# The first pair of each feed-forward stage by eight plain products, late token sums, and filters at full width

## The reference

```python
def encoder_layer(x, lp):
    x = x + 0.5 * swiglu(rms_norm(x, lp['norm_ffn1']), lp['ffn1_w_in'], lp['ffn1_w_out'])
    h = rms_norm(x, lp['norm_mix'])
    proj = h @ lp['w_in']
    ...
    x = x + mixed @ lp['w_out']
    x = x + 0.5 * swiglu(rms_norm(x, lp['norm_ffn2']), lp['ffn2_w_in'], lp['ffn2_w_out'])
    return x

def swiglu(x, w_in, w_out):
    gate, up = jnp.split(x @ w_in, 2, axis=-1)
    return (jax.nn.silu(gate) * up) @ w_out

def hyena_filters(seq_len, lp):
    ...
    h = jnp.sin(freq * (z @ lp['hy_ff_w1'].astype(f32) + lp['hy_ff_b1'].astype(f32)))
    h = jnp.sin(freq * (h @ lp['hy_ff_w2'].astype(f32) + lp['hy_ff_b2'].astype(f32)))
    h = (h @ lp['hy_ff_w3'].astype(f32)).reshape(seq_len, 2, HY_ORDER, C_DIM)
    ...
    h = h * jnp.exp(-t * jnp.abs(deltas))[:, None, None, :]
    h_fwd, h_bwd = h[:, 0], h[:, 1]
    kern = jnp.concatenate([h_fwd, jnp.zeros((1, HY_ORDER, C_DIM), f32), jnp.flip(h_bwd[1:], axis=0)], axis=0)
    return kern / jnp.sum(jnp.abs(kern), axis=0, keepdims=True)
```

## Time and profile before

| | |
|---|---|
| median of 3 executions | 3457.19 us (3455.61 to 3460.02) |
| the profiled execution | 3455.17 us, of which the span is 3453.4 us |
| PE busy | 3263.6 us, 95% of the span |
| DVE, ACT, POOL busy | 2488.0, 1316.1, 74.9 us |
| matmuls of the pairs (L1064) | 7392 in three groups of 2464 |
| mean granted clock of TensorE | 0.984 of full speed |

### The profile page before, as it was taken

The page is one execution under the profiler, slowest core; times in us unless marked ns, Lnnn a source line. Parts: engine busy times, 40 slices in busy tenths (PEclk is TensorE's granted clock), DMA queues, the critical chain, the costliest instruction groups (busy, mean ns, idle before and its releaser), DMA issues.

```text
span 3453.4 us, 63597 instructions
## 1 busy us (share of the span) xinstructions
PE 3263.6 (95%) x25876; PEld 3063.6 (89%) x25876; DVE 2488.0 (72%) x4660; ACT 1316.1 (38%) x2491; POOL 74.9 (2%) x112
## 2 busy tenths in 40 slices
PE   5999999999898999999989999999999978999998
PEld 5899999888776989999979999998877768999997
DVE  7777777663878677667887777776548776776666
ACT  5333334221445343333543333351234535333333
POOL 0001000000000000000000000000000000000000
PEclk8999999999999999999999999999999999999999
DMA  2222222222033112222212222232310512222222
...
DMA packets 89553, 268.15 MB, mean 78 GB/s; under 512 B 10184, under 2 KB 18376, under 8 KB 87984
## 3 DMA queue, kind: packets, MB, share of 16 engines
...
## 4 chain that ended last, share of the span: by engine, by line
PE 81%; DVE 13%; issue 3%; ACT 2%; DMA 1%; SPq 0%; DVEq 0%; POOL 0%; ACTq 0%
PE ps L980 47%; PE ps L1064 34%; DVE uv L2809 1%; DVE wl L2288 1%; DVE gated L2334 1%; DMA wring<-wa 1%; DVE x L2196 0%; DVE rstd L2158 0%; DVE ps L2323 0%; DVE silu L2324 0%; PE ps L1528 0%; DVE gl L2427 0%; DVE gated L2329 0%; DVE wl L2149 0%; DVE act_low L2340 0%
## 5 line engine op out<-in xcount | busy, mean ns | idle before, releaser
L1064 PE MATMUL ps<-gh,wh 128*128 128x384 f32 x2464 | 833.5, 338 | 63.6 <-DVE wl L2288 25.9
L1064 PE MATMUL ps<-gl,wh 128*128 128x384 f32 x2464 | 829.6, 337 | 0.0
L1064 PE MATMUL ps<-gh,wl 128*128 128x384 f32 x2464 | 829.4, 337 | 0.0
L1064 PEld LDWEIGHTS ps<-gh,wh 128*128 128x128 f32 x2464 | 467.5, 190 | 73.0 <-DVE wl L2288 21.8
L980 PE MATMUL ps<-act_high,wh 128*128 128x384 f32 x1408 | 482.0, 342 | 11.3 <-DVE act_low L2340 11.1
L980 PE MATMUL ps<-act_high,wl 128*128 128x384 f32 x1408 | 473.0, 336 | 0.0
L980 PE MATMUL ps<-act_low,wh 128*128 128x384 f32 x1408 | 472.9, 336 | 0.0
L1064 PEld LDWEIGHTS ps<-gl,wh 128*128 128x128 f32 x2464 | 467.4, 190 | 0.4
L1064 PEld LDWEIGHTS ps<-gh,wl 128*128 128x128 f32 x2464 | 467.3, 190 | 0.0
L2196 DVE SCALAR_TENSOR_TENSOR x<-ps,x 128x384 f32<-128x384 f32 x416 | 229.2, 555 | 227.6 <-PE ps L980 227.2
L1661 ACT CAST wh<-wring 128x512 fp32r<-128x512 f32 (+2 forms) x260 | 182.9, 706 | 455.8 <-PE ps L980 368.4
...
## 6 DMA issues: line engine op xcount, KB each, us to landing
wring<-wa SPq DMA_DIRECT2D x244, 512.0 KB, 3.5
wring<-wa SPq DMA_DIRECT2D x128, 256.0 KB, 2.6
...
bias<-bias SPq DMA_DIRECT2D x24, 512.0 KB, 7.6
...
table<-hyc POOLq DMA_DIRECT2D x12, 512.0 KB, 4.0
kern_rows<-kst POOLq DMA_DIRECT2D x24, 256.0 KB, 3.1
outT<-x SPq DMA_DIRECT2D x2, 3072.0 KB, 9.7
```

The source lines that it names most:

```text
L1064: m = pe.matmul(out, lhs[a], rhs[b], start=start and n == 0, stop=stop and n == 2, skip_group_check=onto)
```

## The change

- The first pair of each stage, and all three pairs of the first block in stage 1, is made by eight plain products (`eight`, `plain_product`, `plain_pair`): two of each of four units of weights (the halves of the gate and up tiles as they are, no sums), with B11, T1, B2 and B2. The first half of the tokens leaves the bank as it is; the second adds the held product of B11.
- T2 (with T4's sum), T3 and T4 are made during the first pairs (`LATE_SUMS`): in stages 2 to 4 behind products 4 and 6 of the first pair and behind product 1 of the second, in stage 1 in its second and third pair. T3 no longer comes from T2 but from x and the scaled first tokens, which ACT makes again ("z").
- The filters are made for both orders at once, 256 columns wide: half as many jobs, at new places; sums of magnitudes go to bank 0, kernels to banks 2 and 3; `kst` and `kodd` lie where `silu1` and `gated1` are. `table` lies where `small` and the masks are, so these are loaded in each layer after the last filter, behind the store of x. At the start the second tile of weights is loaded after x.
- Waits are by name of the event instead of by a count worked out from the number of the pair; PE's wait for `small` at L1615 is not touched.

```diff
+def eight(l, f, j):
+
+    return j < (FF_BLOCKS[0][1] if l + f == 0 else 1)
+
+
+def units_of(l, f, j):
+    return 4 if eight(l, f, j) else UNITS
+
+
+def products_of(l, f, j):
+    return 8 if eight(l, f, j) else UNITS
...
-    jobs = [(0, ("mlp", 1)), (4, ("mlp", 2)), (4, None)]
-    for h, o, s in TAP_GROUPS:
-        jobs += [(1, ("taps", h, o, s, p)) for p in TAP_TILES[s][::2]] + [(3, ("sum", h, o, s))]
-        jobs += [(4 if n else 1, ("kern", h, o, a)) for n, a in enumerate(KERN_ORDER[o, s])]
+    jobs = [(2, ("mlp", 1)), (4, ("mlp", 2)), (3, None)]
+    for h, s in TAP_GROUPS:
+        jobs += [(1, ("taps", h, s, p)) for p in TAP_TILES[s][::2]] + [(3, ("sum", h, s))]
+        jobs += [(5 if n else 1, ("kern", h, a)) for n, a in enumerate(SEG_FOLDS[s])]
     out, at = {}, 0
     for gap, job in jobs:
         at += gap
-        if at % 16 > 13:
+        if at % 16 > 12:
...
+        def eight_banks(l, f, j):
+
+            return (4, 5, 6, 7) if j % 2 else (0, 1, 2, 3 if l + f == 0 else 6)
+
+        LATE_SUMS = {(0, 0, 1, 4): "T2", (0, 0, 1, 6): "T3", (0, 0, 2, 4): "T4"}
+        for l_, f_ in PASSES[1:]:
+            LATE_SUMS.update({(l_, f_, 0, 4): "T2", (l_, f_, 0, 6): "T3", (l_, f_, 1, 1): "T4"})
+        PLAIN_LEAD = (3, 3, 3, 3, 5, 5, 6, 6)
+        PLAIN_PARTS = (0, 1, 3, 5)
+        PLAIN_NAMES = ("B11", "T1", "B2", "B2")
...
+            def load_small(l):
+                sp.wait_ge(*fp.at(l, *FILTER_JOBS[-1]))
                 sp.dma_start(small[:, :], small_d[l]).then_inc(s_small, 16)
+                sp.dma_start(cs("masks"), const_d[:, COFF["masks"]:COFF["masks"] + 512]).then_inc(s_masks, 16)
...
                 sp.dma_start(x[:, i:KT:KH, :], xT[:, i:KT:KH, :]).then_inc(s_x[i], 16)
-                if i == 0:
-                    load_tile(1)
-            sp.dma_start(cst[:, :], const_d).then_inc(s_const, 16)
+            load_tile(1)
             load_tile(2)
-            sp.dma_start(small[:, :], small_d[0]).then_inc(s_small, 16)
+            sp.dma_start(cst[:, 512:], const_d[:, 512:]).then_inc(s_const, 16)
...
                 sp.wait_ge(s_xup, x_count(l, 0) + FF_OUTS)
                 sp.dma_start(outT, x[:, :, :]).then_inc(s_spill, 16)
+                load_small(l)
...
                         for dr in range(2):
-                            lo = CHH * (2 * dr + o)
-                            m = mm(ps[:, p % 2, CHH * dr:CHH * dr + CHH], h1[0:64, fold_tokens(p)], hwt[0:64, lo:lo + CHH])
-                        m.then_inc(*fp.inc(l, "taps", h, o, p))
+                            c = slice(2 * CHH * dr, 2 * CHH * dr + 2 * CHH)
+                            m = mm(ps[:, p % 2, c], h1[0:64, fold_tokens(p)], hwt[0:64, c])
...
+            def plain_product(l, f, j, p):
+
+                i, c = p // 2, p % 4
+                pe.wait_ge(*ul.at(l, f, j, i))
+                high, low = unit_part(wh, l, f, j, i), unit_part(wl, l, f, j, i)
+                for k in range(KH):
+                    if j == 0:
+                        pe.wait_ge(*eg.at(2 * l + f, k, PLAIN_NAMES[c]))
+                    gh, gl, _, at = pair_part(k, PLAIN_PARTS[c])
+                    m = mm3_onto(bank(eight_banks(l, f, j)[p // 4 * 2 + p % 2], HALF), (high[:, k, :], low[:, k, :]),
+                                 (gh[:, at, :], gl[:, at, :]), k == 0 and c < 2, k == KH - 1, c > 1)
+                m.then_inc(*pr.inc(l, f, j, p))
+
+            def banks_left(l, f, j, *last):
+
+                pe.wait_ge(*ex.at(l, f, j, *(last or ("u1" if eight(l, f, j) else "u0",))))
+
+            def plain_pair(l, f, j):
+                if pair_before(l, f, j) and pair_before(*pair_before(l, f, j)):
+                    banks_left(*pair_before(*pair_before(l, f, j)))
+                for p in range(8):
+                    if f and p in (0, 1, 4):
+                        pe.wait_ge(s_xup, x_count(l, 2) + 13 + p // 2 + p % 2)
+                    if l + f + j and p == 5:
+                        pe.wait_ge(s_root, norms[0])
+                    if p in (2, 6):
+                        pe.wait_ge(*hd.at(l, f, j, p // 4))
+                    plain_product(l, f, j, p)
+                    if j == 0 and p == (3 if l + f else 7):
+                        norm()
+
+            def seven_pair(l, f, b, j):
+                banks_left(*pair_before(*pair_before(l, f, j)))
+                if j % 2:
+                    pe.wait_ge(s_xup, x_count(l, f) + 16 * b)
+                for i in range(UNITS):
+                    if i == 2:
+                        pe.wait_ge(*hd.at(l, f, j, 0))
+                    if i == 4:
+                        pe.wait_ge(*hd.at(l, f, j, 2))
+                    if i == 6:
+                        pe.wait_ge(*ex.at(l, f, j, "u1"))
+                    product(l, f, j, i)
...
+            def plain_pair(l, f, b, j, q):
+                for p in range(8):
+                    if l + f + j or p > 3:
+                        items_to(l, f, q + PLAIN_LEAD[p])
+                    if p == 0 and j > FF_BLOCKS[b][0]:
+                        act_high1(l, f, b, j - 1, 1)
+                    if p in (0, 4) and l + f + j:
+                        hold(l, f, j, p // 4)
+                    if p == 1 and j == 0 and l + f:
+                        norm()
+                    if p in (3, 4):
+                        silu_of(l, f, j, p - 3)
+                    if (l, f, j, p) in LATE_SUMS:
+                        late_sums(2 * l + f, LATE_SUMS[l, f, j, p])
+                act_high1(l, f, b, j, 0)
+
+            def seven_pair(l, f, b, j, q):
+                first = j == FF_BLOCKS[b][0]
+                order = (1,) if not first and eight(l, f, j - 1) else (1, 0) if not first else ()
+                for t in order[:1]:
+                    act_high1(l, f, b, j - 1, t)
+                for i in range(UNITS):
+                    items_to(l, f, q + i + LEAD)
+                    if i < 3:
+                        hold(l, f, j, i)
+                    if i == 0:
+                        for t in order[1:]:
+                            act_high1(l, f, b, j - 1, t)
+                    if (l, f, j, i) in LATE_SUMS:
+                        late_sums(2 * l + f, LATE_SUMS[l, f, j, i])
+                    if i == 4:
+                        silu_of(l, f, j, 0)
+                silu_of(l, f, j, 1)
...
                     copy_second(g, i)
-                    for name in ("T2", "T3", "T4"):
-                        sum_high(g, i, name)
                     square(p, 0, KH + i)
                 else:
-                    if g > 1 or i:
-                        sa.wait_ge(*(eg.at(g, i - 1, "T4") if i else eg.at(g - 1, KH - 1, "T4")))
+                    sa.wait_ge(*(et.at(g, i - 1, "T1") if i else et.at(g - 1, KH - 1, "T3")))
                     copy_first(g, i)
                     square(p, 0, i)
                     sum_high(g, i, "T1")
+
+            def late_sums(g, name):
+
+                for i in range(KH):
+                    if name == "T3":
+                        sa.wait_ge(*(et.at(g, i - 1, "T3") if i and g else et.at(g, KH - 1, "T1")))
+                        A(first_tokens(g, i), x[:, i, HALF:T], ACT.Copy, scale=gain_of(g, i)).then_inc(*ey.inc(g, i, "z"))
+                    sum_high(g, i, name)
 
 
...
+            def plain_exit(l, f, j, name, b):
+
+                side, t = "gu".index(name[0]), int(name[1])
+                ve.wait_ge(*pr.at(l, f, j, 4 * side + 2 + t))
+                if t:
+                    ve.wait_ge(*hd.at(l, f, j, side))
+                    step(TT(bank(b, HALF), bank(b, HALF), held[side][:, :], AD))
+                to = (silu1, gated1)[side]
+                TT(to[:, t, :], bank(b, HALF), rstd[:, t * HALF:(t + 1) * HALF], M).then_inc(*ex.inc(l, f, j, name))
+                ve.wait_ge(*ex.at(l, f, j, name))
...
+            def last_exit(l, f, j):
+
+                if eight(l, f, j):
+                    plain_exit(l, f, j, "u1", eight_banks(l, f, j)[3])
+                    gate_up(l, f, j, 1)
+                else:
+                    first_up(l, f, j, 3 * (j % 2))
+                    gate_up(l, f, j, 0)
+
+            def last_lows(l, f, b, j):
+                for t in (0, 1) if eight(l, f, j) else (1, 0):
+                    act_low1(l, f, b, j, t)
+
+            def plain_pair(l, f, b, j, q):
+                first, banks = j == FF_BLOCKS[b][0], eight_banks(l, f, j)
+                for p in range(8):
+                    if p == 0 and not first:
+                        last_exit(l, f, j - 1)
+                    if l + f + j or p > 3:
+                        items_to(l, f, q + PLAIN_LEAD[p])
+                    if p == 0 and not first:
+                        last_lows(l, f, b, j - 1)
+                    if p == 3 and j == 0:
+                        norm()
+                    if p == 3:
+                        plain_exit(l, f, j, "g0", banks[0])
+                    if p == 4:
+                        plain_exit(l, f, j, "g1", banks[1])
```

(22 more changed lines are left out.)

552 lines of the change are left out of this document (261 added, 291 removed).

## The result

| | before | after |
|---|---|---|
| median, on one chip | 3456.4 us (3454.75 to 3460.02, 4 runs) | 3486.65 us (3484.69 to 3488.74, 4 runs) |
| ratio to the kernel before | | 1.0081 (95% interval 1.0069 to 1.0093) |
| span of the profiled execution | 3453.4 us | 3487.0 us |
| PE, DVE busy | 3263.6, 2488.0 us | 3267.7, 2443.3 us |

The change costs 0.8%, 30 us. DVE has 45 us less to do and PE 4 us more, and neither number tells the result. The waits do. These are lines of the page after: the chain that ended last, by engine, and two groups (line, engine, operation, output and inputs, count; busy time and mean; idle time ahead and what ended most of it). They answer to the earlier trace rows.

The account below looks back on a forecast made before the run. PE's own work and its gaps bound the kernel (PE 95% busy). Terms +9.7 - 0.4 + 6.7 + 4.5 + 26.2 - 17.0 = +29.7 gave 3484.9 us for the profile, forecast 3486 beside the median; range 3458 to 3502.

Parts of the forecast that it names:

- The small table: Before the first projection: `small` lands behind the spill of x; 11.1 us wait plus 2.0 restart, 26.2 in both layers.
- Rival A: Before the first projection: `small` lands ahead of the spill and doesn't hold PE up; total 3460, chance 0.06.
- The hold in stages 2 to 4: Third product of the second pair: PE waits 11.0 us for ACT's hold behind DVE's queue; +9.7, -0.4, +6.7 by stage.
- The drop of the clock: First three pairs of stages 2 to 4: one period at the low clock in each stage, 1.9 us.
- rival B: Second pair's hold, and third pair in stage 1: late sums are hidden, exits passed 11.5 us after root; 3439, chance 0.11.
- the round trip: T3 job: ACT scales, DVE sums, ACT casts through one buffer before the next scaling; 1.8 us a tile, 7.2 in all.
- Stage 1: First block: earlier start at 16.7, more products and new waits; 93.4 us against 88.92, +4.5.
- waits for B2's low parts: First pair of stage 1: PE waits for DVE's low parts, 0.93 us each, 2.6 us in all.
- Filters: Filter blocks, both layers: full-width jobs save 8.5 us a layer, 17.0 in all; kept range -8 to -24.
- Groups of filter products and the slow step behind them: Filter blocks: 16 fewer groups at 0.26 us save 4.2; 16 fewer slow output starts at 0.12 save 2.0.
- Waits: Filter blocks, per layer: hwt -3.2, x -1.5, magnitudes' sum -0.6; second taps product +1.0 and +1.2, one sum +0.8.
- rival C: Ends of blocks 1 and 2: wide filter jobs hold DVE, next pair's lows late; 4 to 5 us a block, 3504, chance 0.10.

## Why the prediction was right, and where its steps were not

**The small table: right.** Said: it lands behind the store, 11.1 us of wait and 2.0 of restart a layer, 26.2 in all. Measured: 11.33 and 11.09 us of wait, released by the DMA of `small`, the clock at 0.50 behind them, and 28.3 us (26 by the ratios) come back when the table is issued early. Rival A is out in both ways: the table doesn't land ahead of the store, and the run with the two in the other order shows that this order is the cause. The Trainium skill, "DMA: Bandwidth & Descriptors", section "Queues, rings and completion order", says that completion is not first in, first out for an issuing engine. No run here shows such a case: `small` and the store landed as they were issued, in both orders, and the full time of the store counted.

**The hold in stages 2 to 4: right in size, wrong in one cause.** Said 62.7 us for the first three pairs with a wait of 11.0; measured 63.2, 63.1, 63.4 with 11.04, 11.03, 11.03. (The drop of the clock behind the wait was put at 1.9 us and took 2.6: 17 matmuls at a granted clock of 0.50.) Stage 3 lost its 6.0 us wait and paid 11 for it, so its time stays. The queue was counted rightly (exits of the first pair, then act_high, cast, hold), and rival B is out: the last exit ended 21.4 us after the root (counted: 20.9), not within 11.5. The step that failed is the round trip. I put its 1.8 us a tile on the single buffer that ACT may only fill again when its cast is done. The run with four buffers took 0.1 us from the wait; the one with the sums first took 2.8. The 0.58 us in which DVE stands in each tile are the trip sum, cast, low part, in DVE's own order. The buffer's own round trip is there, 1.71 us a tile, but DVE's order alone takes 1.66, so that taking away the first changes nothing. That the two are nearly equal is why the sum came out right: luck in that step, not insight.

**Stage 1: over-sized.** Said +4.5, measured -1.2, or -0.1 with the 1.1 us that the first output product waits longer (said 1.4). The start (17.09, said 16.7), the wait for the first cast (5.16, said 5.3) and the third pair's (6.14, said 6.3) hold. The hold of the second pair is 1.16 instead of 3.0. And 17.09 + 24 x 2.08 + 1.4 + 5.16 + 1.16 + 6.14 = 80.9, which leaves 6.8 us to 87.71 for what I put at 2.6 + 6.8 = 9.4, the second half's low parts and four drops of the clock. The windows tell the two apart, the first matmuls and the whole first pair:

```profile
17.09:22.69 5.60, 5.60 (x17) 5.60 (x18) 5.60 (x11) 5.44 (x9) 0.00 (x0) 1.00 0.03 5
17.09:36.44 19.35, 19.35 (x97) 19.31 (x97) 16.51 (x27) 13.63 (x19) 0.00 (x0) 1.00 0.18 55
```

PE is never idle in the first pair. So the 2.6 us of waits for B2's low parts are the term that was wrong, at 0, together with 1.8 of the 3.0 for the hold, and the slow starts are the 6.8 us that I gave them, though not evenly: 2.7, 1.9, 0.3 and 2.0.

**Filters: under-delivered, and in part by another way than said.** Said -8.5 a layer; measured -5.9 (the -4.8 of the table without those 1.1 us) and -7.6. Groups of filter products and the slow step behind them: said -4.2 - 2.0 = -6.2, measured -5.7 - 0.6 in layer 1 and -4.5 - 0.5 in layer 2, where one wide taps group fell into a stretch at the low clock (3.71 us instead of 1.93). The size is nearly right, and that is luck in part. The 0.11 us that I read for a matmul of 128 columns holds. What stands beside the columns of a taps group is 0.20 us, not 0.26, and merging two kernel groups saves nothing of that kind: there the saving is the width and the 0.4 us of slow steps at the one-row product, which I had not seen in the rows. The rule that I held against my reading, the Trainium skill, "TensorE: Matmul & The Clock Gate", section "Back-to-back issue gap" (2.5 ns beside the columns of an isolated matmul), is not contradicted by the plain steps, 2 x 0.111 - 0.215 = 0.007 us; it leaves out the steps at the ends of the groups and at the one-row product. Waits: said -3.2 - 1.5 - 0.6 + 1.0 + 1.2 + 0.8 = -2.3, measured from 7.97 to 7.31 us in layer 1 and from 6.53 to 5.69 in layer 2, -0.7 and -0.8. The wait for hwt went. But the wait for x ahead of the second block, which I had shrunk by 1.5, stayed at 2.3 (1.7 in the second layer), and the wait for DVE's taps grew from 1.2 to 2.8 (1.7 in the second layer): both are one backlog of DVE, as the shifted taps job shows, and I had counted a gain at the one without seeing it come back at the other. The rest, about +1.4 and -1.7 us, are matmuls at the low clock behind waits, for which I had no term: in layer 1 behind the longer waits at 90.86 and 119.63, while in layer 2 those behind the wait for hwt are gone. Of rival C there is nothing: no low part of a unit is late at the ends of the blocks.

**The sum.** Said +29.7, measured +33.6 between the spans and +30.2 between the medians. Stage 1 was put 4.6 us too high and the filters 3.5 us too good, which nearly cancel: that is luck. The three later stages cost 1.6 us more than said, and the two stretches from the last output products to the end of the mixing 29.4 instead of 26.2, of which some 4 are the scatter of the profiled execution. Waits of 11 us, in five places, are the result.
